# A one-core two-block network: the modulation chunks of the first norm fetched as 0, 2, 1, 3 around three weight tiles, and three column groups opened together

## The reference

```
silu(c) @ w_mod[0] + b_mod[0]  -> shift 1, scale 1, gate 1, shift 2, scale 2, gate 2   (1024 each)
h  = rms_norm(x,   norm1[0]) * (1 + scale 1) + shift 1          # x:   512 tokens
hc = rms_norm(ctx, norm1[0]) * (1 + scale 1c) + shift 1c        # ctx: 256 tokens
proj = h @ fh_w_in;  projc = hc @ fh_w_in                       # 1024 -> 2048
u_f = proj[:, :512] -> 2-D Fourier transform
u_h = depthwise_conv3(proj[:, 512:])
a filter from three small layers: sin(f * (z @ w1 + b1)), sin(...), sin(...), then @ w4
```

## Time and profile before

| what | value |
|---|---|
| median of three runs | 3414.77 us (3411.88 to 3416.74) |
| span of the profiled execution | 3412.4 us |
| TensorE busy | 3261.6 us, 96% of the span |
| DVE, ACT, POOL busy | 1418.5, 1307.4, 1393.8 us |
| mean DMA rate | 84 GB/s |
| mean granted TensorE clock | 0.982 of full |

### The profile page before, as it was taken

One profiled execution on the slowest core, in us unless ns is written; L12 is line 12 of the kernel. 1 busy time (PEld: TensorE's weight loads), 2 busy tenths in 40 slices (PEclk: granted clock), 3 DMA queues, 4 the chain that ended last, 5 costly groups with the idle time before them and its releaser, 6 DMA issues.

```text
span 3412.4 us, 40303 instructions
## 1 busy us (share of the span) xinstructions
PE 3261.6 (96%) x16296; PEld 2583.0 (76%) x16296; DVE 1418.5 (42%) x2558; ACT 1307.4 (38%) x2311; POOL 1393.8 (41%) x788
## 2 busy tenths in 40 slices
PE   7989999999999889999999999999999999999998
PEld 4864788888875456788886688888887768878887
DVE  5556342222246664321222757243232658434132
ACT  4221342212235666432333534353333443444243
POOL 2223432322343334444463036544455215554445
PEclk9989999999999999999999999999999999999999
DMA  6134223121222000423232021332323111122322
GB/s 229 62 115 180 103 86 130 56 74 45 63 83 85 13 13 10 141 84 112 84 115 99 19 79 28 104 104 84 109 86 118 51 43 60 43 90 90 108 84 71
DMA packets 85638, 286.08 MB, mean 84 GB/s; under 512 B 9771, under 2 KB 10347, under 8 KB 84940
## 3 DMA queue, kind: packets, MB, share of 16 engines
q1 hardware_dynamic: 85452, 283.50, 25.4%
HBM read 281.37 MB, written 2.10 MB: 83 GB/s over the span
## 4 chain that ended last, share of the span: by engine, by line
PE 87%; DVE 7%; ACT 4%; DMA 1%; issue 1%; POOL 0%; SPq 0%; DVEq 0%; ACTq 0%
PE ps L459 20%; PE ps L462 20%; PE ps L460 20%; PE ps L1999 2%; PE ps L499 2%; PE ps L501 2%; PE ps L500 2%; PE ps L529 1%; DMA ring<-in_w_mod 1%; PE ps L2069 1%; PE ps L1226 1%; PE ps L437 1%; PE ps L2043 1%; PE ps L2394 1%; PE ps L438 1%
## 5 line engine op out<-in xcount | busy, mean ns | idle before, releaser
L411 POOL TENSOR_TENSOR WL<-ring,WH 128x1024 fp32r<-128x1024 f32 (+2 forms) x443 | 961.4, 2174 | 1520.3 <-ACT WH L402 1519.9
L459 PE MATMUL ps<-HX,WH 128*128 128x512 f32 x1768 | 695.4, 393 | 3.0 <-POOL WL L411 3.0
L462 PE MATMUL ps<-HX,WL 128*128 128x512 f32 x1768 | 692.4, 392 | 0.0
L460 PE MATMUL ps<-HX,WH 128*128 128x512 f32 x1768 | 690.5, 391 | 0.0
L402 ACT CAST WH<-ring 128x1024 fp32r<-128x1024 f32 (+2 forms) x443 | 420.2, 950 | 371.0 <-PE ps L462 312.9
L459 PE MATMUL ps<-FR,WH 128*128 128x512 f32 x1120 | 419.1, 374 | 0.3
L460 PE MATMUL ps<-FR,WH 128*128 128x512 f32 x1120 | 409.7, 373 | 0.0
L459 PEld LDWEIGHTS ps<-HX,WH 128*128 128x128 f32 x1768 | 332.5, 188 | 82.5 <-issue 7.4
L462 PE MATMUL ps<-FR,WL 128*128 128x512 f32 x1120 | 389.4, 373 | 0.0
L462 PEld LDWEIGHTS ps<-HX,WL 128*128 128x128 f32 x1768 | 333.6, 189 | 49.9
L460 PEld LDWEIGHTS ps<-HX,WH 128*128 128x128 f32 x1768 | 332.8, 188 | 49.0
(11 more groups left out here) (391 smaller groups left out, 5096.7 us busy)
## 6 DMA issues: line engine op xcount, KB each, us to landing
ring<-in_w_mod SPq DMA_DIRECT2D x96, 512.0 KB, 5.5
ring<-in_ffn_w_up SPq DMA_DIRECT2D x88, 512.0 KB, 3.4
ring<-in_w_up SPq DMA_DIRECT2D x88, 512.0 KB, 3.3
ring<-in_w_in_tok SPq DMA_DIRECT2D x40, 512.0 KB, 3.4
ring<-in_w_in_feat SPq DMA_DIRECT2D x32, 512.0 KB, 3.3
ring<-in_ffn_w_down SPq DMA_DIRECT2D x32, 384.0 KB, 3.1
ring<-in_w_out SPq DMA_DIRECT2D x32, 384.0 KB, 3.2
ring<-in_w_down SPq DMA_DIRECT2D x32, 384.0 KB, 3.1
```

Source lines behind the costliest of these rows:

```text
L411: pool.tensor_tensor(WL[:, p % SPLITS, 0:n], ring.ap(r), WH[:, p % SPLITS, 0:n], ALU.subtract).then_inc(*ring.frees(r, split.g, "low", p))
L459: pe.matmul(o, high, xh, first, False)
L460: pe.matmul(o, high, xl, False, False)
L462: m = pe.matmul(PS[bs[i]][:, 0:N], low, get(k)[0], False, last)
```

## The change

The chunks are fetched and multiplied as 0, 2, then 1, 3. The three weight tiles of the first three groups come into the list between them: two ahead of chunk 2, one behind it. The norm's parts, factors and low halves are made for k = 0 to 3 once chunks 0 and 2 are there, for k = 4 to 7 once chunks 1 and 3 are there. The first three groups are opened together (`front=3`). Chunks 1 and 3 are multiplied and turned inside that loop, ahead of the passes (k, x) that the function `upper` names. Their six banks are kept from other takers meanwhile. The load of the masks and DVE's cast of them move from the start to later; ACT casts all three weight tiles, and POOL subtracts all three, ahead of the parts.

```diff
-        def pair_pe(pe, L, ins, pair):
+        def pair_pe(pe, L, ins, pair, before=lambda k, x: None):
...
+            held = [b for _, _, bs, _ in opened for b in bs]
+            bank.kept.update(held)
             for k in range(pair[0].kt):
                 c = slice(k * 128, k * 128 + 128)
-                for g, streams, bs, p in opened:
+                for x, (g, streams, bs, p) in enumerate(opened):
+                    before(k, x)
...
-        PLACE = {c: i for i, c in enumerate((*range(0, 10), 12, 13, 14, 15, 10, 11, *range(17, 20), 16, *range(20, 24)))}
+        PLACE = {c: i for i, c in enumerate((0, 2, 1, 3, *range(4, 10), 12, 13, 14, 15, 10, 11, *range(17, 20), 16, *range(20, 24)))}
...
+        def rows_of(c):
+            return [ring.raw(dr["w_mod"][c // 12][c % 12][q], 1024) for q in range(4)]
...
-        def scales_v(dve, i, name, part):
+        def scales_v(dve, i, name, part, k0=0, k1=8):
...
-            for j, (k, s) in enumerate(items):
+            for j in range(k0 * nst, k1 * nst):
+                k, s = items[j]
...
-                      front=2)
+                      front=3, before=before)
...
+                if n == 12:
+                    act.wait_ge(*st0.v.at("masks"))
...
-            side = adaln_pe(pe, range(0, 4))
+            side = adaln_pe(pe, (0, 2))
             next(side)
-            next(side)
+            ring.ask(2)
             for s, name in enumerate(("n0x", "n0c")):
                 first_sums_pe(pe, name, (S, SC)[s], s)
-            next(side)
-            ring.ask(2)
             last_of(side)
             ring.ask(SPLITS)
+            slots = {c: rows_of(c) for c in (1, 3)}
             ring.here("inputs")
-            in_pe(pe, filter_pe(pe))
+
+            def upper(k, x):
+                if (k, x) == (1, 1):
+                    rows_pe(pe, 1, slots[1])
+                elif (k, x) == (2, 0):
+                    turned_row_pe(pe, 1)
+                elif (k, x) == (2, 2):
+                    rows_pe(pe, 3, slots[3])
+                elif (k, x) == (3, 1):
+                    turned_row_pe(pe, 3)
+
+            in_pe(pe, filter_pe(pe), upper)
...
-            dve.wait_ge(*lds["masks"])
-            dve.tensor_copy(masks[:, :], buf(20480, 640).bitcast(I32)).then_inc(*st0.v.up("masks"))
...
-            last_of(adaln_v(dve, range(0, 4)))
-            scales_v(dve, 0, "norm1", 1)
-            parts_v(dve, "n0", sts)
+            for k0, chunks in ((0, (0, 2)), (4, (1, 3))):
+                last_of(adaln_v(dve, chunks))
+                scales_v(dve, 0, "norm1", 1, k0, k0 + 4)
+                parts_v(dve, "n0", sts, False, k0, k0 + 4)
+            dve.wait_ge(*lds["masks"])
+            dve.tensor_copy(masks[:, :], buf(O_VV, 640).bitcast(I32)).then_inc(*st0.v.up("masks"))
...
-            side = adaln_a(act, range(0, 4))
+            side = adaln_a(act, (0, 2, 1, 3))
             next(side)
-            next(side)
+            cast_to(act, 1)
             for q in sts:
                 root_a(act, q.name, q.N, q.r)
             next(side)
-            cast_to(act, 1)
+            cast_to(act, SPLITS - 1)
+            parts_a(act, "n0", sts, False, 0, 4)
             last_of(side)
-            parts_a(act, "n0", sts)
-            cast_to(act, SPLITS - 1)
+            parts_a(act, "n0", sts, False, 4, 8)
...
-            rest_to(pool, 1)
+            rest_to(pool, SPLITS - 1)
             parts_g(pool, "n0", mod_streams("n0", 0, 0, "norm1"))
-            rest_to(pool, SPLITS - 1)
```

More of the change, by code:

```diff
@@ L441, in pair_pe @@
                         m.then_inc(*split.pe.up("used", p))
+            bank.kept.difference_update(held)
         def unit_pe(pe, L, g, unit, streams, bs, order=None):
@@ L463, in unit_pe, with linear_pe @@
             m.then_inc(*split.pe.up("used", p))
-        def linear_pe(pe, L, ins, beside=None, groups=None, front=0):
+        def linear_pe(pe, L, ins, beside=None, groups=None, front=0, before=lambda k, x: None):
             groups = L.groups if groups is None else groups
             if front:
-                pair_pe(pe, L, ins, groups[:front])
+                pair_pe(pe, L, ins, groups[:front], before)
                 for _ in range(front):
@@ L523, in rows_pe @@
             for q in range(4):
-                r = ring.raw(dr["w_mod"][c // 12][c % 12][q], 1024)
+                r = slots[q] if slots else ring.raw(dr["w_mod"][c // 12][c % 12][q], 1024)
                 pe.wait_ge(*ring.landed(r))
@@ L554, in added_v, with turned_row_pe @@
                               ALU.add).then_inc(*bank.emptied(key, mod.v, "added", c))
+        def turned_row_pe(pe, c):
+            b = bank.take("mod_t", c)
+            pe.wait_ge(*bank.free("mod_t", c))
+            turned_pe(pe, c, b, 0)
         def adaln_pe(pe, chunks):
             def turned(c):
-                b = bank.take("mod_t", c)
-                pe.wait_ge(*bank.free("mod_t", c))
-                turned_pe(pe, c, b, 0)
+                turned_row_pe(pe, c)
             before = None
@@ L605, in some_v @@
             added_v(dve, ("mod_n", c0), c0, n)
-        def scales_v(dve, i, name, part):
+        def scales_v(dve, i, name, part, k0=0, k1=8):
             dve.wait_ge(*mod.v.now())
             for s in range(2):
-                d = sm[:, 80 + 8 * s:88 + 8 * s]
-                dve.scalar_tensor_tensor(d, mods[i][:, part * 8:part * 8 + 8, s], 1.0,
-                                         pv[:, PCOLS[name] + 8 * i:PCOLS[name] + 8 * i + 8],
+                d = sm[:, 80 + 8 * s + k0:80 + 8 * s + k1]
+                dve.scalar_tensor_tensor(d, mods[i][:, part * 8 + k0:part * 8 + k1, s], 1.0,
+                                         pv[:, PCOLS[name] + 8 * i + k0:PCOLS[name] + 8 * i + k1],
                                          ALU.add, ALU.mult).then_inc(*nm.v.up())
@@ L713, in part_d, with parts_v @@
             return sts[s].src(k) if inplace else T[:, 2 + j % 4, 0:sts[s].N]
-        def parts_v(dve, name, sts, inplace=False):
+        def parts_v(dve, name, sts, inplace=False, k0=0, k1=8):
             items = part_items(sts)
@@ L741, in parts_v, with parts_a @@
                                          ALU.mult).then_inc(*up)
-                if j >= nst:
+                if k > k0:
                     low(j - nst)
-            for j in range(len(items) - nst, len(items)):
+            for j in range((k1 - 1) * nst, k1 * nst):
                 low(j)
-        def parts_a(act, name, sts, inplace=False):
+        def parts_a(act, name, sts, inplace=False, k0=0, k1=8):
             items = part_items(sts)
-            for j, (k, s) in enumerate(items):
+            for j in range(k0 * len(sts), k1 * len(sts)):
+                k, s = items[j]
                 q, d = sts[s], part_d(sts, j, k, s, inplace)
@@ L988, in in_dst, with in_pe @@
             return fbuf((O_U, O_X0, O_X1, O_VV)[n // 4], n % 4, s)
-        def in_pe(pe, beside):
+        def in_pe(pe, beside, before):
             sts = mod_streams("n0", 0, 0, "norm1")
             linear_pe(pe, L_in, lambda g: [(halves[s], (S, SC)[s], parts_done("n0", sts, s)) for s in range(2)], beside,
-                      front=2)
+                      front=3, before=before)
             next(beside, None)
@@ L3246, in sync @@
             sp.dma_start(CX[:, :, :], dr["ctxT"]).then_inc(*lds["cx"])
-            sp.dma_start(buf(20480, 640).bitcast(I32), dr["masks"]).then_inc(*lds["masks"])
             for r in range(len(ring.order) + 1):
@@ L3250, in sync @@
                     if name == "inputs":
+                        sp.dma_start(buf(O_VV, 640).bitcast(I32), dr["masks"]).then_inc(*lds["masks"])
                         sp.dma_start(rows[:, :], dr["rows"]).then_inc(*lds["rows"])
```

2 lines of the change are left out of this document (1 added, 1 removed).

## The result

The changed kernel takes 3417.14 us (median of 20 runs, 3413.04 to 3422.74), the kernel before 3412.49 us (20 runs, 3407.97 to 3416.74). The ratio is 1.0016, with a 95% interval of 1.001 to 1.0023: a loss of 4.6 us by the medians, 3.4 to 7.8 us by the interval. The forecast had 3420.8 us, counted from a median of three runs of the kernel before (3414.77); over 20 runs that median is 2.3 us lower. Of the kernel before, two of the 15 runs taken beside one later experiment were slow ones (over 11800 us) and are left out there. The profiled execution has a span of 3416.0 us, where the kernel before had 3412.4.

What follows compares the result with a forecast made beforehand. The prediction took TensorE to bound the kernel nearly throughout. Start -9.0, modulation +6.0, wait at k = 4 +1.1, bank +5.9 and clock +2.0 gave +6.0 us, 3420.8 us; range 3415 to 3426.

Steps and rivals of the forecast that it cites:

- The start: First in-projection matmul at 35.5 us, 9.0 us sooner than before.
- POOL's subtraction holding DVE up for 1.4 us: Before the start, weight tile 2's subtraction delays DVE's factors; between 0 and 1.4 us, taken as 1.4.
- In the loop: Multiplying and turning two chunks now stands on TensorE's path, 6.0 us; the loop ends at 70.0.
- The wait at k = 4: In the loop, TensorE runs out of passes at 56.3 and waits for chunk 3 until 57.4: 1.1 us.
- the rival in which it falls a third time: The wait at k = 4 lowers the clock within the loop: +1.6, total +7.6; chance with other added waits 0.32.
- Behind the loop: Group 3 waits for group 1's bank, copied behind ACT's sine; it begins at 77.3, bank term +5.9 us.
- the bank is no wait: Rival: group 1's copies precede the sine, TensorE waits only for the weight tile at 72.3: -1.0 us, chance 0.05.
- The clock: After some 5.9 us idle ahead of group 3, the clock is low, costing 2.0 us.
- The sum: The difference at group 3, low clock included: +6.0 us; as summed, +4.5 to +6.8, chance 0.38.
- I carry the difference to the end: Behind group 3's start both programs are alike, so the +6.0 us there is taken as the whole difference.

Runs made afterwards that it cites:

- copies first: The changed kernel with ACT copying group 1 out of its banks ahead of the filter's first sine instead of behind it: 3412.49 us, ratio 1.0000.
- all repairs: The changed kernel with group 1's copies ahead of the sine, weight tile 2 later, and tile 3 cast ahead of group 0's copies: 3410.13 us, ratio 0.9997.

## Why the prediction was right or wrong

**The start: right, the 0.05 us by luck.** Forecast 35.5, measured 35.45; six profiles whose programs are alike up to there start at 34.33 to 35.68. The step on which I took the upper end of an unknown cost, POOL's subtraction holding DVE up for 1.4 us, was the right choice: line 623 took 2.05 us and ended with POOL's operation, and 0.23 us where POOL was elsewhere. The Trainium skill, page "SBUF — State Buffer", on the separate sides of the memory, says that the later of two such operations waits for the whole of the other; the trace agrees, even for four columns: 2.05 us beside POOL's operation, 0.23 without it.

**In the loop: right, the sizes a little high.** From their first matmul to the next of a pass, rows took 1.86 us a chunk and turnings 0.81, together 5.3 us and not 6.0: a group's printed duration (1.92 and 0.95) overlaps the next start. The pass behind each was 0.1 us longer, which gives 0.4 back. The wait at k = 4 was 0.84 us against 1.1, and the clock stayed at 1.00 there: the rival in which it falls a third time didn't happen, though it did in two of the three profiles in which this wait was 1.88 or 1.90 us. The loop ended at 69.83 (forecast 70.0). By these terms it would be 35.45 + 25.4 + 2.0 + 5.7 + 0.84 = 69.4. The other 0.4 us is in the first pass behind the wait, which took 1.46 us (56.74 to 58.20) and not 1.06. Its context half waited for POOL's low half (line 782, 56.64 to 57.69), a second wait at k = 4 that the forecast has no term for:

```profile
57.74 0.39 PE L440 MATMUL ps<-HC,WH 128*128 128x256 f32 x1
```

**Behind the loop: right.** Group 3 began at 77.44 (77.3), after a wait of 6.11 us ended by line 1019. From the layer to group 3 it took 7.6 us and not 7.3, and the loop ended 0.2 us sooner: two small misses that cancel in part. That DVE's first step on the layer (line 918 before, 930 now) is no longer beside POOL holds too: it took 0.42 us. The experiment with the copies first shows that without this order on ACT the wait is gone. It is the case of the rival "the bank is no wait": that one had TensorE wait for the weight tile until 72.3 (measured 72.22) and end 1.0 us ahead of the kernel before. Measured was a difference of 0.1 us either way, by the medians and at the transposes, since 1.1 us went to the new wait ahead of layer 1.

**The clock: right in kind, too high.** Forecast 2.0 us, measured 1.3 by the run that kept TensorE busy. In the second profile of the changed kernel group 3 took 88.67 - 78.34 = 10.33 us, so 1.8, and with tile 2 later and with the masks first 10.18 and 10.37. Four profiles with this wait thus lost 1.3 to 1.8 us. The upper end of the forecast's 1.5 to 2.1 came from a misread place: near 3051 the clock was still at 1.00 when TensorE resumed and fell only at about 3052.5 (0.74 from 3052 to 3053, 0.50 up to 3055, then 0.56 and 1.00). It was low for 3.4 us and not 4.2, which costs 1.7.

**The sum: right, a little high.** +6.0 was forecast at group 3 with its clock, +5.4 was measured at layer 1 and again at the transposes (198.32 against 192.92), and +4.6 by the medians, whose interval of 3.4 to 7.8 holds all of these. In the first profiles group 3 began 0.1 us later than forecast, and the clock behind it cost 0.7 less: that is the difference at layer 1, and the term mis-sized most is the clock's. The second profiles have +7.0 at the transposes (199.70 against 192.74), so that the forecast lies between the two pairs is in part luck.

**The step that failed: "I carry the difference to the end".** Within a profile the difference isn't carried. It is +5.4 at the transposes, +0.2 at 310 us, -1.25 at the start of the out-projection's loop and +4.2 at 430 us, though the instructions are the same. The +4.6 of the medians can thus be held against the sum only in so far as this averages out over the 20 runs of each. Two things are seen there. First, the clock: the windows of the kernel before

```profile
190.00:350.00 160.00, 146.87 (x634) 85.48 (x635) 100.00 (x128) 36.08 (x68) 55.23 (x37) 0.91 0.47 172
```

and of the changed kernel

```profile
190.00:350.00 160.00, 141.13 (x641) 82.23 (x639) 102.28 (x128) 38.30 (x71) 56.90 (x37) 0.96 0.47 174
```

show a granted clock of 0.91 and 0.96 over nearly the same work, 29 and 14 us at the lower level. Second, a wait that takes it back, in TensorE's timeline of the changed kernel:

```profile
346.65 0.47 PE L440 MATMUL ps<-HX,WH 128*128 128x512 f32 x1
...
350.60 0.77 PE L440 MATMUL ps<-HX,WH 128*128 128x512 f32 x1 [2.65 <-DVE mod L558]
```

It is there again in its second profile (2.27 us), and in the second profile of the kernel before it is

```profile
348.29 0.47 PE L437 MATMUL ps<-HX,WH 128*128 128x512 f32 x1 [0.32 <-DVE mod L551]
```

TensorE got to this place sooner than DVE, which adds the modulation's bias behind work of its own that POOL stretches. DVE did so at 350.30 and 352.32 in the two profiles of the changed kernel, at 348.87 and 347.99 in those of the kernel before: TensorE's lead of 1.25 us in the first profile was worth nothing there, and in the second one it waited without a lead. Over the whole mixer the stretch took 227.1 to 235.2 us in twelve profiles, without an order that follows the edits: 227.8 and 231.0 for one program. Low clock from 190 to 350 us goes with it only in part (14.0 us at the lower level with 234.0, 13.6 with 227.1), because it leaves out the waits and what is behind 350 us. Read from windows over the whole stretch, with TensorE's idle time and half of the time at the lower clock taken off, 201.7 to 204.8 us are left in all twelve (changed: 19.5 idle and 22.4 at the lower level; copies first: 16.1 and 15.3). So most of the spread is waits and low clock. Why they fall out differently in each execution isn't settled by these runs. Two profiles of one kernel lie 1.4 to 3.0 us apart in span, as much as some edits are worth, so the forecast is held against the medians.

## What to carry to other kernels

When several groups of an accumulation are opened together, look at which bank the next group inherits and at what stands ahead of that bank's read-out on its engine: a copy that nobody waited for had a sine ahead of it that waits for DVE, and cost 6.1 us and then the clock once TensorE came round to it. Work that lay in the shadow of a transfer gets its full price when the transfer is no longer waited for, so count it into the sum before calling an earlier start a gain (9.1 us gained, some 6 spent on that and the wait at k = 4). An edit of a few microseconds in 3400 has to be read at an anchor shortly behind it, but behind the clock's return ("all repairs" lost 1.5 us of its lead just behind layer 1), in more than one profile, and by medians of many runs, not by the span of one profile.

## What was not expected of the hardware

- Two DVE operations of 128x4 with two SBUF inputs, beside POOL's subtraction of 2.34 us, took 2.05 us together, 0.23 without it; one of 64x256 took 2.50 against 0.42; one of 128x512 took 2.85 against 0.75. Each ended 0.1 to 0.6 us behind POOL's operation, whatever its own size. When the first meeting was removed, POOL's operation met another of DVE's some four microseconds later, and 0.6 of the 1.8 us won at the start were gone by layer 0.
- Two profiles of one program differed by 1.4 us at the transposes, since the clock came back at different moments after the same idle stretches (group 3: 9.86 and 10.33 us, 8.58 at the full clock).
- Between the loop's start and group 4, waits of TensorE up to 1.13 us left the clock at 1.00 in every profile. Waits of 1.83 to 1.90 us (one ahead of layer 1, three at k = 4) were followed by the lower clock in three of four cases, each at a cost of some 1.5 us or more.
- From 190 to 350 us, over nearly the same matmuls, the time at the lower clock was 13.6 to 29.4 us in twelve profiles, with 13.6 and 20.4 for one program.
